# Modulation blocks of the next layer loaded by GpSimd's queue, weight tiles by the sync queue alone

## The reference

```python
def adaln(cvec, w, b, n):                  # c: 1024 values, w: 1024 x 6144
    m = jax.nn.silu(cvec) @ w[:, : n * D_MODEL] + b[: n * D_MODEL]
    return jnp.split(m, n, axis=-1)        # shift, scale, gate, twice

def _conv_ffn(h, w_up, conv_w, conv_b, w_down):
    gate, val = jnp.split(h @ w_up, 2, axis=-1)
    gate = conv_of_width_3(gate, conv_w) + conv_b
    return (jax.nn.silu(gate) * val) @ w_down      # 1024 -> 2 x 2816 -> 1024
```

## Time and profile before

| | |
|---|---|
| median of 3 runs | 3584.64 us (3579.1 to 3585.17) |
| span of the profiled execution | 3586.9 us |
| TensorE busy | 3398.5 us, 95% |
| VectorE busy | 2036.2 us, 57% |
| ScalarE busy | 1316.4 us, 37% |
| GpSimd busy | 426.0 us, 12% |
| blocks on the sync queue | 144 of 512 KB, 3.4 us to landing (median) |
| moved by the sync queue's DMAs | 304.13 MB |
| moved by GpSimd's DMAs | 14.71 MB |

### The profile page before, as it was taken

The page is one execution under the profiler, slowest core; times in us unless marked ns, Lnnn a source line. Parts: engine busy times, 40 slices in busy tenths (PEclk is TensorE's granted clock), DMA queues, the critical chain, the costliest instruction groups (busy, mean ns, idle before and its releaser), DMA issues.

```text
span 3586.9 us, 47397 instructions
## 1 busy us (share of the span) xinstructions
PE 3398.5 (95%) x18907; PEld 2761.9 (77%) x18907; DVE 2036.2 (57%) x3206; ACT 1316.4 (37%) x1974; POOL 426.0 (12%) x387
## 2 busy tenths in 40 slices
PE   7998999999989889999999879999999999999998
PEld 5776788888877667787787557888888766678886
DVE  3766456535557655868624766663555565564355
ACT  4346332212224454323233554321222545444233
POOL 2004450000000140000001551000000023300000
PEclk9999999999999999999999999999999999999999
DMA  5440133434412103555421012343342211123332
GB/s 183 141 136 13 43 70 106 131 94 130 132 56 72 46 17 96 175 160 175 124 64 48 18 37 60 106 130 105 112 136 76 56 36 32 31 73 103 91 103 72
DMA packets 477242, 321.87 MB, mean 90 GB/s; under 512 B 54872, under 2 KB 450558, under 8 KB 477024
## 3 DMA queue, kind: packets, MB, share of 16 engines
q1 hardware_dynamic: 467104, 304.13, 28.6%
q0 software_dynamic: 9920, 14.71, 1.6%
HBM read 313.20 MB, written 3.57 MB: 88 GB/s over the span
## 4 chain that ended last, share of the span: by engine, by line
PE 82%; DVE 7%; ACT 5%; DMA 3%; issue 3%; POOL 0%; SPq 0%; DVEq 0%; ACTq 0%; POOLq 0%
PE PS L1072 78%; PE PS L1384 3%; DMA RAW<-in_w_gate 1%; DVE CPROD L2702 1%; DVE TMP L2465 1%; ACT SPH L1692 1%; DVE HL L2449 1%; ACT BIG L1901 1%; DVE ATT L2536 1%; ACT TMP L1827 1%; DMA RAW<-in_w_in 0%; DMA XSTG<-in_x 0%; ACT HH L1830 0%; DVE CACC L2781 0%; ACT PTR L1879 0%
## 5 line engine op out<-in xcount | busy, mean ns | idle before, releaser
L1072 PE MATMUL PS<-HH,SPH 128*128 128x512 f32 (+1 forms) x3424 | 1174.1, 356 | 42.1 <-ACT SPH L1692 14.7
L1072 PE MATMUL PS<-HL,SPH 128*128 128x512 f32 (+1 forms) x3424 | 1133.7, 354 | 8.1 <-DVE HL L2449 7.4
L1072 PEld LDWEIGHTS PS<-HH,SPH 128*128 128x128 f32 x3424 | 649.7, 190 | 162.2 <-issue 33.4
L1072 PE MATMUL PS<-HH,SPL 128*128 128x512 f32 (+1 forms) x3424 | 738.3, 355 | 0.0
L1072 PEld LDWEIGHTS PS<-HL,SPH 128*128 128x128 f32 x3424 | 642.3, 190 | 101.6 <-DVE HL L2449 15.5
L2297 DVE TENSOR_TENSOR SPL<-RAW,SPH 128x1024 fp32r<-128x1024 f32 (+3 forms) x367 | 458.3, 1249 | 391.8 <-ACT SPH L1692 391.2
L1072 PEld LDWEIGHTS PS<-HH,SPL 128*128 128x128 f32 x3424 | 579.2, 190 | 97.9 <-issue 7.4
L1692 ACT ACTIVATE SPH<-RAW 128x1024 fp32r<-128x1024 f32 (+3 forms) x367 | 394.1, 1074 | 663.0 <-PE PS L1072 432.6
L1072 PE MATMUL PS<-MH,SPH 128*128 128x512 f32 (+1 forms) x1056 | 362.5, 356 | 3.8 <-ACT SPH L1692 3.8
L1072 PE MATMUL PS<-ML,SPH 128*128 128x512 f32 (+1 forms) x1056 | 359.7, 355 | 0.0
L2637 DVE SCALAR_TENSOR_TENSOR X<-PS,MOD,X 128x512 f32<-128x512 f32 (+1 forms) x144 | 95.3, 662 | 365.1 <-PE PS L1072 363.3
(11 more groups left out here) (339 smaller groups left out, 3564.1 us busy)
## 6 DMA issues: line engine op xcount, KB each, us to landing
MS<-in_mod_turned SPq DMA_DIRECT2D x144, 512.0 KB, 3.4
RAW<-in_l_w_up SPq DMA_DIRECT2D x88, 512.0 KB, 3.9
RAW<-in_w_gate SPq DMA_DIRECT2D x44, 512.0 KB, 4.6
RAW<-in_w_val SPq DMA_DIRECT2D x44, 512.0 KB, 4.6
RAW<-in_w_down SPq DMA_DIRECT2D x32, 704.0 KB, 5.7
RAW<-in_l_w_down SPq DMA_DIRECT2D x32, 704.0 KB, 5.2
RAW<-in_w_in SPq DMA_DIRECT2D x40, 512.0 KB, 4.6
MS<-in_w_mod SPq DMA_DIRECT2D x32, 512.0 KB, 4.8
```

Of the source, the lines that this page charges most:

```text
L1072: return pe.matmul(o, a, b, start=start, stop=stop)
```

## The change

The loads of the blocks leave the sync queue's program and become one loop on GpSimd's queue, with semaphores of their own (block_landed). The loop for layer li's 48 blocks stands where GpSimd has loaded the first row tile and the conditions of the next layer, and in layer 0 behind the bias rows. The second row tile comes behind the loop. The loop waits first for the first tile of w_out, since MS lies over the attention's buffers, and then before each block for the sum of block m-2, as before. The sync queue keeps its wait for the same tile and loads weight tiles only. TensorE's and ScalarE's programs are as before. VectorE's differs in the semaphore on which a sum waits.

```diff
--- before.py
+++ after.py
@@ -391,6 +391,7 @@
             param_landed = [sem("param_landed0"), sem("param_landed1")]
             x_landed = [sem("x_landed"), sem("ctx_landed")]
             ms_landed = [sem("ms_landed0"), sem("ms_landed1")]
+            block_landed = [sem("block_landed0"), sem("block_landed1")]
             bias_landed = [sem("bias_landed0"), sem("bias_landed1")]
         block = ctx.enter_context(nc.Block())
 
@@ -862,16 +863,6 @@
                     src = layers[0]["w_ada"][512 * (m % 2):512 * (m % 2) + 512, 256 * (m // 2):256 * (m // 2) + 256]
                     sp.dma_start(MS[m % 2][:], src.rearrange("(k p) c -> p k c", p=P)).then_inc(S.ms_landed[m % 2], 16)
 
-            def load_blocks(li, half, name, j):
-
-                for m in blocks_with(li, half, name, j):
-                    if m < 2:
-                        sp.wait_ge(S.mod_done, 48)
-                    if 48 * li + m >= 2:
-                        sp.wait_ge(S.mod_summed, 48 * li + m - 1)
-                    sp.dma_start(MS[m % 2][:].rearrange("p k c -> p (k c)"), d["mod_turned"][li, m * P:(m + 1) * P, :])\
-                        .then_inc(S.ms_landed[m % 2], 16)
-
             def load_bias(p):
 
                 slots = biasd.rearrange("(u i) (b r n) -> i u b (r n)", u=4, b=2, n=16)
@@ -910,7 +901,6 @@
                     for x, name in zip(L["ffn"][half], ("up", "down")):
                         def load_ffn(j, t, s, x=x, name=name, half=half):
                             load(x, j, t)
-                            load_blocks(li, half, name, j)
                         tiles(x, load_ffn)
 
             for j, (by_dve, by_act) in enumerate(((4, 0), (5, 0), (3, 2), (0, 3))):
@@ -1004,18 +994,30 @@
                 for c in range(3, DC):
                     pool.tensor_tensor(X[:, c, 0:T], X[:, c, 0:T], HLF[:, 7, 0:T], ALU.add).then_inc(S.shifted, 1)
 
+            def load_blocks(li):
+
+                pool.wait_ge(S.tile_done, layers[li]["w_out"].t0 + 1)
+                if li == 0:
+                    pool.wait_ge(S.mod_done, 48)
+                for m in range(48):
+                    if 48 * li + m >= 2:
+                        pool.wait_ge(S.mod_summed, 48 * li + m - 1)
+                    pool.dma_start(MS[m % 2][:].rearrange("p k c -> p (k c)"), d["mod_turned"][li, m * P:(m + 1) * P, :])\
+                        .then_inc(S.block_landed[m % 2], 16)
+
             for li, L in enumerate(layers):
                 blk, l = L["blk"], L["l"]
                 if li:
 
                     pool.wait_ge(S.rope_free, w.seen(S.rope_free))
                     load_rows(2 * li + 1)
-                    load_rows(2 * li + 2)
                     if li < 4:
                         for v, c in enumerate((d["c"][0], d["c_ctx"]) if li == 1 else (d["c_2"][0], d["c_ctx_2"])):
                             pool.dma_start(CB[:, v, :], c.partition_broadcast(P)).then_inc(S.cond_landed, 16)
                     if li == 1:
                         fill_bias()
+                    load_blocks(li - 1)
+                    load_rows(2 * li + 2)
                     if blk == 1 and l == 0:
                         up = layers[li - 1]["ffn"][1][0]
                         pool.wait_ge(S.tile_done, up.t0 + up.n)
@@ -2694,7 +2696,7 @@
 
                 for m in blocks_with(li, half, name, j):
                     dve.wait_ge(S.cond_ready, li + 1)
-                    dve.wait_ge(S.ms_landed[m % 2], 16 * (16 + 24 * li + m // 2 + 1))
+                    dve.wait_ge(S.block_landed[m % 2], 16 * (24 * li + m // 2 + 1))
                     nv = conds_of(li + 1, m)
                     for v in range(nv):
                         done = S.mod_summed if v == nv - 1 else S.dve_step
```

## The result

The changed kernel takes 3564.1 us (median of 4 runs, 3559.9 to 3565.5), where the kernel before takes 3584.9 (4 runs, 3579.1 to 3587.6) beside it. The ratio is 0.9939, with an interval of 0.9925 to 0.9953: 20.8 us less. The spans of the profiled executions are 3586.9 and 3563.7 us, at a granted clock of 0.990 and 0.991.

A forecast was written before the change was run, and what follows sets the result against it. TensorE held 82% of the chain, but layer 1 waited for w_gate loads queued behind blocks. Terms of -5.8, -6.1, -2.6 and -2.7 sum to -17.2 us, from 3584.64 to 3567.4, stated as 3568; range 3561 to 3581.

The forecast's parts named there:

- a sentence on the clock: Layer 1's pairs: granted clock read as 1.00, the 2.4 GHz level, so the clock was taken to play no part.
- the size of the pair: Gate and value up tiles in layer 1: 12.05 us falls to 11.34, VectorE's work from split to split, not TensorE's 10.86.
- the landing on GpSimd's queue: Blocks loaded by GpSimd land in 4 to 6.5 us, within 8.8 us of room, so they cost nothing.
- half 0, 7 pairs: Layer 1, first half: 7 pairs go from 85.15 us to 79.4 at 11.34 each, -5.8 us.
- half 1, 9 pairs: Layer 1, second half: 9 pairs go from 108.15 us to 102.1 at 11.34 each, -6.1 us.
- sum to down tile, half 0: Layer 1, first half: first down tile starts 1.8 us after the last even sum instead of 4.4, -2.6 us.
- sum to down tile, half 1: Layer 1, second half: first down tile starts 1.8 us after the last even sum instead of 4.6, -2.7 us.
- the cover of 35 us: Context tokens staged behind layer 1's blocks: after an 11.9 us landing, 35 us stay before they are needed; no cost.
- A: Rival in layer 1: ScalarE and VectorE overlap more closely, TensorE keeps its floor, up to 23 us go, 3562; chance 0.12.
- B: Rival: blocks land late on GpSimd's queue; at 11.9 us a layer 1 pair takes 14.5, +44 us, 3629; chance 0.08.
- C: Rival: each GpSimd issue, about 0.55 us, holds VectorE up; layer 1 pair 12.44 us, 3587, no measurable change; chance 0.06.
- D: Rival: the load was not what counted in layer 1, landings stretch, half the gain stays away, about 3577; chance 0.06.

## Why the prediction was right, point by point

The forecast was 3568 with a range of 3561 to 3581. Measured were 3564.1, and 20.8 us of gain against 17.2. The mechanism was right. What the forecast had wrong is a sentence on the clock, the size of the pair by 0.09 us, and the landing on GpSimd's queue.

**Where the gain is.** Layer 1 gives 20.07 us. VectorE's sums, the counterparts of the earlier trace rows (first and last of half 0, then of half 1), give it term by term.

```profile
1423.83 1.22 DVE L2704 CUSTOM_DVE_ANT_0 CPROD<-MS,CB 128x1024 f32<-128x1024 f32 x1 [0.17 <-DVE SM L3008]
...
1502.59 1.23 DVE L2704 CUSTOM_DVE_ANT_0 CPROD<-MS,CB 128x1024 f32<-128x1024 f32 x1 [0.17 <-DVE SM L3008]
...
1583.55 1.22 DVE L2704 CUSTOM_DVE_ANT_0 CPROD<-MS,CB 128x1024 f32<-128x1024 f32 x1 [0.17 <-DVE SM L3008]
...
1685.18 1.23 DVE L2704 CUSTOM_DVE_ANT_0 CPROD<-MS,CB 128x1024 f32<-128x1024 f32 x1 [0.17 <-DVE SM L3008]
```

The last column sets the changed kernel against the other profile with the old order in layer 1, that of the run with layers 0 and 2 changed alone (sums at 1422.53, 1506.39, 1590.31 and 1698.29, down tiles at 1511.04 and 1702.62, layer 2 at 1823.49).

| term | forecast us | measured us | from | against the other profile |
|---|---|---|---|---|
| half 0, 7 pairs | -5.8 | -6.39 | 78.76 for 85.15 | -5.10, for 83.86 |
| half 1, 9 pairs | -6.1 | -6.52 | 101.63 for 108.15 | -6.35, for 107.98 |
| sum to down tile, half 0 | -2.6 | -2.71 | 1.69 for 4.40 | -2.96, for 4.65 |
| sum to down tile, half 1 | -2.7 | -2.87 | 1.70 for 4.57 | -2.63, for 4.33 |
| from that down tile on, not foreseen | 0 | -1.57 | 120.13 for 121.70, below | -0.74, for 120.87 |
| sum | -17.2 | -20.06 | layer 1: -20.07 | -17.78, layer 1: -17.77 |

**The pair, mechanism right, size 0.09 us off.** The step was "12.05 less the single wait for ScalarE's SPH of 0.71, so 11.34". The pair takes 11.25. The bracket of an idle time was read as the whole cost of the wait. But VectorE's instructions overlap when nothing hinders them: from the second product to the split is 1.15 us now, and was 1.95, so the wait had cost 0.80. At 0.09 us a pair, 16 pairs make 1.4 us. The first two terms missed by 1.0, since one pair of half 1 takes 11.60: the sum at 1640.16 starts after 0.53 us of idle time where the others have 0.17. The same place shows 0.52 or 0.53 us in the other profiles with this order and this table of blocks, and what holds it there is not shown.

**The load left late, and now leaves at once.** Right: 0.03 us after the split against a forecast of within 0.1. VectorE's waits in layer 1 (1395 to 1705 before, 1390 to 1700 after: us, times, longest) name what went.

Before:

```profile
DVE SPL L2297 <- ACT SPH L1692: 26.5, 29, 2.6
```

After:

```profile
DVE SPL L2299 <- ACT SPH L1694: 10.9, 8, 2.3
```

The 8 waits that stay are in tiles without blocks: in the stretch from 1400 to 1500 four of them, and none once the sums run. "VectorE no longer waits for SPH" was true of the pairs that it spoke of.

**The missed term.** In half 1 the stretch from the first down tile into layer 2 became 1.57 us shorter, though its work is the same. The first 132 matmuls alone took 31.80 us and now take 30.22. TensorE in the kernel before, at that place (timeline):

```profile
1707.19 0.51 PE L1072 MATMUL PS<-MH,SPH 128*128 128x512 f32 x1 [2.10 <-ACT SPH L1692]
...
1708.35 0.63 PE L1072 MATMUL PS<-ML,SPH 128*128 128x512 f32 x1
1708.78 0.63 PE L1072 MATMUL PS<-MH,SPH 128*128 128x512 f32 x1
```

After, the first rows of the same tile:

```profile
1686.88 0.50 PE L1074 MATMUL PS<-MH,SPH 128*128 128x512 f32 x1 [0.36 <-ACT SPH L1694]
1687.21 0.39 PE L1074 MATMUL PS<-ML,SPH 128*128 128x512 f32 x1
1687.44 0.40 PE L1074 MATMUL PS<-MH,SPH 128*128 128x512 f32 x1
```

Before, they follow each other by 0.43 us, and after by 0.23. The granted clock is the number ahead of the DMA share in these stretches, all of the kernel before (busy us of PE, PEld, DVE, ACT, POOL; clock, DMA share, GB/s):

```profile
1707.10:1709.00 1.90, 1.81 (x5) 1.49 (x6) 1.83 (x2) 0.04 (x1) 0.00 (x0) 0.62 1.04 341
1709.00:1711.00 2.00, 2.00 (x6) 1.54 (x6) 1.19 (x4) 1.56 (x2) 0.00 (x0) 0.51 1.02 370
1711.00:1716.40 5.40, 5.40 (x26) 4.46 (x25) 3.66 (x5) 1.74 (x2) 0.00 (x0) 1.00 0.67 215
```

So after an idle time of 2.10 us TensorE came to run at half its clock, the 1.2 GHz level, until about 1711, and lost 1.6 us. In the changed kernel it waits for 0.36 us and keeps 1.00 from there through the first four down tiles.

The same happened once more in the kernel before, in half 0. A load of w_gate took 5.68 us (the one at 1470.52), TensorE waited for 1.88 us, and the clock fell 1.5 us later. The 24 matmuls of that up tile took 7.40 us on the chain, where those at 1645.17 took 5.79. The chain, TensorE's timeline and the clock there:

```profile
1477.33 7.40 PE PS L1072 x24
...
1477.33 0.50 PE L1072 MATMUL PS<-HH,SPH 128*128 128x512 f32 x1 [1.88 <-ACT SPH L1692]
...
1478.80:1482.30 3.50, 3.50 (x10) 2.68 (x10) 2.66 (x6) 1.69 (x2) 0.00 (x0) 0.51 0.37 107
```

Some of the 85.15 us of half 0, which the prediction took for waits alone, was therefore clock. The step that failed is the sentence "The clock is no part of this". It rested on one stretch within the pairs, and the clock had not been read behind the longer waits, neither in half 0 nor at the last one.

The length of a wait does not tell whether the clock falls. In half 0 of the kernel before, the wait ahead of the first down tile was 1.67 us and the clock stayed at 1.00 (1515.2 to 1519). From 1515.21 to the next sum it took 79.26 us, and from 1504.28 now 79.27. In the run with layers 0 and 2 changed alone, the waits ahead of the two first down tiles were as long as those that went with a fall, and the clock stayed at 1.00 behind both (TensorE's timeline, then the stretch behind the second):

```profile
1511.04 0.50 PE L1088 MATMUL PS<-MH,SPH 128*128 128x512 f32 x1 [2.09 <-ACT SPH L1708]
...
1702.62 0.50 PE L1088 MATMUL PS<-MH,SPH 128*128 128x512 f32 x1 [1.97 <-ACT SPH L1708]
...
1702.60:1707.00 4.40, 4.38 (x19) 3.65 (x20) 3.58 (x5) 1.92 (x2) 0.00 (x0) 1.00 1.03 357
```

What decides it, these profiles do not show. In that run the 0.74 us behind the last first down tile have another cause: the second down tile waited too, and started 8.21 us behind the first where 33 matmuls take 7.47.

So of the 20.1 us some 2.3 hang on the clock and the landings of one profiled execution, and 17.8 are the gain over an old order that kept its clock. That the forecast of 17.2 lies so near to the latter is in part luck: its half 0 term was worked out from a stretch that held a clock loss. The medians of the two kernels lie 19.2 to 20.8 us apart in three sets, so the old order may pay for the clock in some of its executions and not in others; two profiles of it don't tell how often. In the other eleven profiles, the changed kernel's among them, no wait of TensorE from 1385 to 1730 is longer than 1.34 us, and the clock stays at 1.00 there. By these profiles the new order doesn't meet the loss.

**GpSimd's queue.** The landing was taken at 4 to 6.5 us and measured 3.6 on 144 blocks, below both. Nearest to it was the row of RTB, 3.8, for the same 512 KB. The CB loads, on which I had leaned for their shape, are pairs issued one behind the other. Room was 8.8 us, so it cost nothing either way. The Trainium skill, "DMA: Bandwidth & Descriptors" (Anatomy of one DMA — SWDGE (gpsimd) path), gives an estimate of 3.2 us by its formula, 0.4 below the trace. On the sync queue the blocks took 3.3 to 3.4.

What now stands behind the blocks was reached later than I had reckoned (GpSimd's timeline):

```profile
1705.89 0.53 POOL L1005 DMA_DIRECT2D MS<-in_mod_turned  x1 [6.31 <-DVE MODN L2704]
1706.41 0.56 POOL L936 DMA_DIRECT2D PSTG<-in_l_conv_w  x1
1706.96 0.75 POOL L924 DMA_DIRECT2D XSTG<-in_ctx  x1
```

The tokens leave at 1706.96, 20 us behind the start of the first down tile, where before it was 1.8 us ahead of it (1705.39 and 1707.19). It was estimated at about 13 behind. They landed 9.5 us later and are wanted behind the eighth down tile, near 1747, so the cover of 35 us was 30, and it held.

**The rivals.** A (TensorE keeps its floor, 3562) did not come: the pair is 11.25 and not 10.86, and only less work on VectorE brings it to 10.87. That its 3562 lies nearer to 3564.1 than my 3568 is chance, since the largest part of the miss is the clock. B (blocks land late) did not come either, and with one buffer it did, at the price shown. C (VectorE pays for the issues): the split at 1448.75 has GpSimd's issue of 1449.12 within it and takes 1.22 us, as without one. This bears on the lock that was named as B's cause. By the Trainium skill, "SBUF — State Buffer" (Who interferes with whom), two-input instructions leave GpSimd's writes alone, and the trace agrees, with landings of 3.6 us and issues of 528 ns beside them. D (half of the gain stays away): w_gate's landing was 4.6 us in layer 1 and is 4.4. It was the load.

## What to carry to other kernels

In a queue that issues in order, a DMA waits for its own buffer and for all the waits ahead of it. Where one load waits for a slow consumer and the next has its buffer free, either exchange them or give one another queue: both gave the same here, 468.46 and 468.47 us of layer 1, and the exchange is an edit of a few lines. Then price the gain at the next engine's own sequence, not at the length of the wait removed, and put work such as these products where the engine has room: beginning two tiles earlier and leaving two up tiles of each half without a block brought back 3.6 us of the 5 that lay between the changed kernel and TensorE alone (463.41 us in layer 1). And read the clock behind each long wait, not in one regular stretch.

## What the runs showed of the hardware

- TensorE's clock fell to half behind idle times of 2.10 and 1.88 us, for some 3.5 us each, and stayed full behind 2.09, 1.97, 1.67 and 0.36 us. So a wait near 2 us on this engine can cost 1.6 us more than its length, or nothing more; the length alone does not decide it.
- A load of 512 KB in 128 rows of 4 KB takes 3.6 us to land from GpSimd's queue and 3.3 to 3.4 from the sync queue (medians), beside weight loads of 4.4 to 4.6. It takes 0.53 us of GpSimd's own time, and some 0.34 of the sync engine's.
- From the end of a sum to the start of the next one that hangs on a reloaded buffer, the landing is not all: the wait until the issue and the start behind the landing added 0.4 us (with one buffer, 6.61 = 2.5 + 3.7 + 0.4).
- Where instructions overlap, an idle time shown in a timeline can be less than what the wait costs: 0.71 us were shown and 0.80 were paid.
